# Neighbourhood attention heads: the scores of two steps issued in one burst, with records of opposite row halves in turn

## The reference, cut to what matters

```python
# 8 heads of width 64; grid of 8 rows x 64 columns, 16 meta keys
s_win = jnp.einsum('bchd,bicjhd->bhcij', q_row, k_win).astype(jnp.float32) * scale
s_win = s_win + bias[None].astype(jnp.float32)
s_meta = jnp.einsum('bchd,bmhd->bhcm', q_row, km).astype(jnp.float32) * scale
s = jnp.concatenate([s_win.reshape(b, NA_HEADS, GRID_W, kh * NA_KW), s_meta], axis=-1)
p = jax.nn.softmax(s, axis=-1).astype(v.dtype)
```

## Time and profile before

| | us |
|---|---|
| median of three runs | 1720.97 |
| lowest, highest | 1715.65, 1722.9 |
| the profiled execution, its own time | 1730.19 |
| span of its trace | 1728.9 |
| TensorE busy | 1651.0 (95% of the span) |
| VectorE, ScalarE busy | 874.0, 621.5 |
| mean granted TensorE clock | 0.973 |

### The profile page before, as it was taken

The page is one execution under the profiler, slowest core; times in us unless marked ns, Lnnn a source line. Parts: engine busy times, 40 slices in busy tenths (PEclk is TensorE's granted clock), DMA queues, the critical chain, the costliest instruction groups (busy, mean ns, idle before and its releaser), DMA issues.

```text
span 1728.9 us, 24772 instructions
## 1 busy us (share of the span) xinstructions
PE 1651.0 (95%) x10349; PEld 1401.1 (81%) x10349; DVE 874.0 (51%) x1560; ACT 621.5 (36%) x1100; POOL 52.5 (3%) x52
## 2 busy tenths in 40 slices
PE   7999989999999999999999998999999999999997
PEld 5897767777888888889888778999988877777886
DVE  4434556556645654945544344336544445434443
ACT  5232244334322333723343342223323344332333
POOL 0000000000000000020000000000110000000000
PEclk9999979999999999999999899999999999989999
DMA  6235300014333322431202201224321112012331
GB/s 189 74 77 105 91 13 13 25 54 125 89 96 98 97 98 86 98 73 50 68 31 63 36 25 62 86 74 135 74 72 51 51 49 74 13 37 74 110 107 51
DMA packets 175599, 125.21 MB, mean 72 GB/s; under 512 B 48752, under 2 KB 172272, under 8 KB 175488
## 3 DMA queue, kind: packets, MB, share of 16 engines
q1 hardware_dynamic: 175488, 123.63, 25.2%
HBM read 121.52 MB, written 2.10 MB: 71 GB/s over the span
## 4 chain that ended last, share of the span: by engine, by line
PE 89%; DVE 4%; ACT 3%; issue 2%; DMA 1%; SPq 0%; POOL 0%; DVEq 0%; ACTq 0%; POOLq 0%
PE bank L576 68%; PE bank L2648 2%; PE bank L2680 2%; PE bank L1581 2%; PE bank L2660 2%; PE bank L2986 2%; PE bank L1540 1%; PE bank L2559 1%; PE bank L3022 1%; PE bank L1467 1%; ACT w_hi L523 1%; PE bank L3001 1%; PE bank L1242 1%; PE bank L2510 1%; DMA na_bias_a<-na_rel 1%
## 5 line engine op out<-in xcount | busy, mean ns | idle before, releaser
L576 PE MATMUL bank<-h_hi,w_hi 128*128 128x512 f32 (+2 forms) x920 | 329.1, 378 | 9.9 <-issue 4.7
L532 DVE TENSOR_TENSOR w_lo<-w_raw,w_hi 128x2048 fp32r<-128x2048 f32 (+2 forms) x117 | 241.2, 2061 | 183.2 <-ACT w_hi L523 183.0
L576 PE MATMUL bank<-h_lo,w_hi 128*128 128x512 f32 (+2 forms) x920 | 324.0, 372 | 0.0
L576 PE MATMUL bank<-h_hi,w_lo 128*128 128x512 f32 (+2 forms) x920 | 322.6, 371 | 0.0
L523 ACT ACTIVATE w_hi<-w_raw 128x2048 fp32r<-128x2048 f32 (+2 forms) x117 | 201.2, 1721 | 67.7 <-DMA w_raw<-w_in 31.2
L576 PEld LDWEIGHTS bank<-h_hi,w_hi 128*128 128x128 f32 (+1 forms) x920 | 167.6, 190 | 55.4 <-issue 21.1
L576 PE MATMUL bank<-g_hi,w_hi 128*128 128x264 f32 (+1 forms) x784 | 197.2, 315 | 3.2 <-DVE g_lo L1693 1.8
L576 PE MATMUL bank<-g_lo,w_hi 128*128 128x264 f32 (+1 forms) x784 | 195.0, 312 | 0.0
L576 PE MATMUL bank<-g_hi,w_lo 128*128 128x264 f32 (+1 forms) x784 | 194.2, 311 | 0.0
L576 PEld LDWEIGHTS bank<-h_hi,w_lo 128*128 128x128 f32 (+1 forms) x920 | 167.5, 190 | 31.0
L576 PEld LDWEIGHTS bank<-h_lo,w_hi 128*128 128x128 f32 (+1 forms) x920 | 167.5, 190 | 29.9 <-issue 0.5
(11 more groups left out here) (561 smaller groups left out, 2626.2 us busy)
## 6 DMA issues: line engine op xcount, KB each, us to landing
w_raw<-w_in SPq DMA_DIRECT2D x45, 1024.0 KB, 5.3
w_raw<-w_up SPq DMA_DIRECT2D x32, 512.0 KB, 4.9
w_raw<-w_in SPq DMA_DIRECT2D x40, 256.0 KB, 4.5
w_raw<-w_down SPq DMA_DIRECT2D x8, 1024.0 KB, 5.2
w_raw<-w_out SPq DMA_DIRECT2D x8, 1024.0 KB, 5.2
w_raw<-w_out SPq DMA_DIRECT2D x8, 512.0 KB, 3.4
w_raw<-w_ple_gate SPq DMA_DIRECT2D x4, 1024.0 KB, 5.2
w_raw<-w_o_attn SPq DMA_DIRECT2D x8, 512.0 KB, 3.4
```

Of the source, the lines that this page charges most:

```text
L532: DV.e.tensor_tensor(wlo[u % RING][:, 0:n], raw[u % RING][:, 0:n], whi[u % RING][:, 0:n].bitcast(F32), ALU.subtract).then_inc(*w_low(u))
L576: ins = PE.e.matmul(out, stationary[a](k), moving[b](k)[i], start=first and n == 0, stop=last and n == 2)
```

## The change

The score stage of TensorE does nothing at odd x, apart from the meta scores of the next tile. At even x it issues the work of steps i and i + 1: first the two masks, into banks 2 and 3, then the four head products in the order lower half, upper half, lower half, upper half. Before them it waits for `a_taken` of step i - 1, the last reader of the second bank, where the old order waited for step i - 2. The last product of each bank raises `a_scored` of its step. All other stages and engines keep their order.

```diff
+                if x % 2:
+                    return
                 k0, kn, m0, which = spans[t]
-                if i > 1:
-                    PE.wait_ge(*a_taken.at(l, i - 2))
-                view = bank[:, 2 + i % 2, 0:2 * kn].rearrange("p (n k) -> p n k", n=2)
-                PE.e.matmul(view, idb[:, :], maskb[:, which, m0:m0 + kn].unsqueeze(1).broadcast_to([P, 2, kn]), start=True,
-                            stop=False, skip_group_check=True)
-                for n, h in enumerate(heads2[x]):
-                    rows = slice(AD * (h % 2), AD * (h % 2) + AD)
-                    ins = PE.e.matmul(view[:, n, :], y.qb[rows, h // 2, t * P:(t + 1) * P], y.kb[rows, h // 2, k0:k0 + kn],
-                                      start=False, stop=True, skip_group_check=True)
-                ins.then_inc(*a_scored(l, i))
+                if i:
+                    PE.wait_ge(*a_taken.at(l, i - 1))
+                views = [bank[:, 2 + side, 0:2 * kn].rearrange("p (n k) -> p n k", n=2) for side in range(2)]
+                for view in views:
+                    PE.e.matmul(view, idb[:, :], maskb[:, which, m0:m0 + kn].unsqueeze(1).broadcast_to([P, 2, kn]), start=True,
+                                stop=False, skip_group_check=True)
+                for n in range(2):
+                    for side in range(2):
+                        h = heads2[x + side][n]
+                        rows = slice(AD * side, AD * side + AD)
+                        ins = PE.e.matmul(views[side][:, n, :], y.qb[rows, h // 2, t * P:(t + 1) * P],
+                                          y.kb[rows, h // 2, k0:k0 + kn], start=False, stop=True, skip_group_check=True)
+                        if n:
+                            ins.then_inc(*a_scored(l, i + side))
```

## The result

The changed kernel takes **1706.15 us** (median of 11 runs, 1700.45 to 1715.4); the kernel before took 1720.33 beside it (11 runs, 1715.16 to 1723.19). The ratio is 0.9917, with a 95% interval of 0.9901 to 0.9933: **14.2 us or 0.83% faster**. Forecast were 1718.5 and a range of 1710 to 1728, so the kernel gained more than the range held.

What follows compares the result with a forecast made beforehand. TensorE, holding 89% of the chain, was taken as the bound. -7.6 us of work and +5.1 for one clock episode gave -2.5, applied to the median 1720.97: 1718.5 us, range 1710 to 1728.

Steps and rivals of the forecast that it cites:

- The burst and the pair: TensorE's scores: eight records take 1.06 us, a pair of steps 1.60 instead of two times 1.37.
- rival 4: Score records of opposite halves don't overlap, a burst takes 2.12 us: +4.7 us, time 1725.7; chance 0.04.
- the semaphore tail: Each pair's last two matmuls both raise a semaphore: 16 times 0.026, an estimated 0.4 us more, left out.
- The three kinds of places: Pairs ahead of dense work swap 1.37 us for 0.23; those ahead of exponentials or another wait lose 0.23.
- rival 5: Saving waited away everywhere, VectorE and ScalarE being late ahead of dense work too: 0 to +1 us, 1721.5; chance 0.13.
- The sum: Full-clock saving over both layers' heads: -3.5 us in layer a, -4.1 in b, together -7.6, bounds -6 and -10.
- The clock takes some back: Longer stops in the heads bring one or two new half-clock episodes, 5.1 us each; one was taken.
- the seven stops: Stops of 1.67 to 2.2 us in the earlier trace, four with lowered clock: odds of about a half.
- rival 3: Slower: half-clock episodes at new stops in sparse tiles cost 8.5 us each; two give +9.5, 1730.5; chance 0.13.
- (1): The saving whole, with no new half-clock episode: -7.6 us, time 1713.4; chance 0.27.
- a lucky clock: One of two ways named for the kernel to gain more than 8.6 us; chance of such a gain 0.23.

Runs made afterwards that it cites:

- one_half: The changed kernel with all score records of a burst on rows 0 to 63: 1725.31 us, ratio 1.0036 to the kernel before.
- before_third: The kernel before, unchanged, run for a third trace; one execution of 1721.57 us.
- after: The changed kernel itself, in its first profiled execution: 1706.15 us.
- after_again: The changed kernel, unchanged, run again for a further trace: 1707.96 us, ratio 0.9929 to the kernel before.
- before_again: The kernel before, unchanged, run for a second trace; one execution of 1713.94 us.
- full_bursts: The changed kernel with all score records on all 128 rows, so nothing overlaps: 1708.37 us, ratio 0.9936 to the kernel before.
- early_pair: The changed kernel with the first pair of tiles t = 1 to 3 given a step earlier: 1703.81 us, ratio 0.9904 to the kernel before.
- chosen_early: The changed kernel, first pair a step earlier only in layer a t = 1 to 3, layer b t = 2, whose steps 10, 11 stay single: 1702.7 us.
- first_pair: The changed kernel with only steps x = 0, 1 of a tile given together, the others singly: 1717.77 us, ratio 0.9996 to the kernel before.
- second_pair: The changed kernel with only steps x = 2, 3 of a tile given together, the others singly: 1713.95 us, ratio 0.9959 to the kernel before.
- rows32: The kernel before with each score record on only 32 rows: 1724.89 us, ratio 1.003 to the kernel before.
- rows_full: The kernel before with each score record on all 128 rows: 1702.67 us, ratio 0.9892 to the kernel before.
- in_blocks: The changed kernel with each burst ordered lower, lower, upper, upper instead of in turn: 1707.71 us, ratio 0.9916 to the kernel before.

## Why the prediction was right and wrong

**The burst and the pair: right.** Eight records 1.07 (forecast 1.06), a pair 1.60 (1.60), in a 192-column tile 1.28 (1.27):

```profile
1004.67 0.50 PE L2985 MATMUL bank<-na_mask,ident 128*128 128x384 bf16 x2
1005.10 0.92 PE L2991 MATMUL bank<-kb_a,qb_a 64*128 64x192 f32 x8
1005.95 0.33 PE L3007 MATMUL bank<-identity,na_probs_a 128*128 128x128 f32 x1
```

Of the 1.14 us that a pair saves in front of dense work, one_half puts 0.86 down to the overlap and 0.28 to one passage fewer between 128-row and 64-row records, a cost that the forecast had inside its 0.31 and 1.06 without naming it; the 0.08 that rival 4 would leave was too low for that reason. Rival 4 (no overlap) is out; the semaphore tail that the forecast left out of the sum can't be told: its 0.4 us would lie within the error.

**The three kinds of places: right.** The stops at x = 0 were 1.72, 1.58 and 1.34 in layer a (forecast 1.75 twice, 1.35), 1.58 and 3.23 in layer b (1.6 to 1.75 and 3.3). At t = 0, which the forecast left out of its new stops, the stop grew too, from 0.84 (before_third) to 1.94 in layer a and 1.97 in layer b; from the start of the heads to its end it is 0.16 and 0.18 us longer, near the 0.17 of the forecast's bound. The chain of waits for the heads of layer a and of layer b in the changed kernel (engine, line, waited for: us, times, longest) names ScalarE and, once, VectorE:

```profile
PE bank L3007 <- ACT na_probs_a L3072: 6.6, 4, 1.9
```

```profile
PE bank L3007 <- ACT na_probs_b L3072: 3.5, 2, 2.0
PE bank L3007 <- DVE o_rows_b L2623: 3.2, 1, 3.2
```

No stop stands ahead of the dense products, which rules out rival 5.

**The sum: right, and closer than it had to be.** -7.7 +- 0.5 against -7.6, with bounds of -6 and -10; that it came within 0.1 is in part luck. Tile t = 1 of layer a gave 0.92 (0.91), the second pairs -6.8 (-6.5). By layer, length times clock of the windows above, as means of after and after_again against before_again and before_third: layer a 69.4 against 73.6, layer b 80.2 against 84.2, -4.2 and -4.0 where I had -3.5 and -4.1. The clock is given to 0.01 there, which is worth 0.4 us in each stretch, so the layers can't be told apart more finely. The first pairs alone came out at +0.1, not -1.1, which lies within twice their error.

**"The clock takes some back": this step failed.** It was +5.1 us for one new episode; the clock gave 5.7 +- 1.1 back. The step read from the seven stops of the earlier trace rows that a stop brings half clock with odds of a half, and priced the new stops at those odds. What it got wrong is the odds and the sign of the rest. (a) Half clock followed 1 of 24 such stops in six traces, and none of the eight in the changed kernel's two. (b) one_half and full_bursts have the same order and nearly the same stops, and their clocks are 0.9769 and 0.9836. (c) early_pair and chosen_early take these stops away, and the clock stays.

What the step had at nothing is how many rows of the array work while TensorE is busy. 32, 64 and 128 rows in one order of instructions give 0.9754, 0.9787 and 0.9842, and the same new order with its records on one half or on both at once gives 0.9769 or 0.9818. The change puts 64 + 64 rows to work together for 1.07 us where 64 rows worked for 2.12. The forecast had the sparse work in sight, but only as what makes an episode last longer (rival 3), and did not ask whether the change makes that work less sparse.

Stops are not out of it. The 17.07 us behind a new stop in first_pair are the forecast's own mechanism, seen once, and they reached 5 us into the dense product, as the episode of the earlier trace rows did (its product starts at 968.78 and it ends at 973.83). All six episodes in the heads of the changed kernel's traces stand at stops of 1.94 us or more, and one_half lies 0.0021 +- 0.0010 below the kernel before. Against that stand the two episodes of the kernel before that began with no stop ahead. Whether a stop begins an episode or only falls together with it, no run here decides.

Of the rivals, (1) was nearest, with its -7.6 and no new episode. It too had no term for a clock that rises, though the forecast gave 0.23 to a gain of over 8.6 us, by a sum near its bound of -10 or "a lucky clock". That left 1710 as the lower bound, above the 1706 that came. The forecast named its weak point itself: a clock of the sparse tiles that behaves in another way than the seven stops suggest.

**What stays open.** Why neither pair alone raised the clock (second_pair, first_pair) and both did; rows in use would let each do a part of it. How much the stops take. And the clock's rise is spread over executions: the 52 runs before and 18 after overlap (from 1709.84 and up to 1715.4 us), and a single pair of profiles would not show it.

## What to carry to other kernels

Where matmuls use half of the array's rows, put two of opposite halves into one burst on two banks: eight float32 records took 1.07 us instead of 1.92. What this saves is worth something only ahead of TensorE work that needs no answer from ScalarE or VectorE; elsewhere give the pair earlier, as chosen_early does, which at 1702.7 beats both kernels. When forecasting at a granted clock below 1, ask what the edit does to the rows in use while TensorE is busy, before pricing stops. Split each run into full-clock time and loss to the clock before judging it: here a gain of 13.4 us in the means was 7.7 of work and 5.7 of clock.

## What the runs showed of the hardware

- The mean granted clock rose with the rows in use: 0.9754, 0.9787 and 0.9842 for 32, 64 and 128 rows in the scores alone, 64 records a layer. That is 15.5 us of difference in what is lost to the clock between the ends, for work that takes some 40 us of 1720 (16 steps of 1.37 and 16 of 1.10).
- Going from 128-row to 64-row records and back costs 0.29 us, once for a step of four records (1.37 against 1.08) and once for a burst of eight (2.46 against 2.17), though the 64-row records do half the work. Contracting over rows that aren't needed, with zeros in them, could thus be quicker; that wasn't tried.
- The written order within a burst of eight does not matter (1.07 us in blocks and in turn).
- Half clock followed 1 of 24 stops of 1.02 to 1.72 us ahead of transposes, and stood at six of six stops of 1.94 us or more in the changed kernel's heads.
- The bias of the neighbourhood heads lands late in some executions, in both kernels' variants. VectorE's waits for it in the kernel before:

```profile
DVE na_probs_a L3133 <- DMA na_bias_a<-na_rel: 3.3, 1, 3.3
```

  and in layer b of second_pair (5.0), rows32 (4.5), first_pair (3.9, and 1.1 in layer a), chosen_early (3.8), early_pair (1.8) and rows_full (1.2): 7 of the 14 traces. The other seven (after, after_again, before_again, before_third, in_blocks, one_half, full_bursts) have none. The 3.3 us are part of why the profiled execution of before lay some 10 us above its median, and a reason to apply a sum to the median and not to a profiled execution.
